# Two fused transformer blocks on one core: a later row piece and sum, stores spread over a stage, and weight chunks at the ends of two attention passes

## The reference

```python
# first block
mod = silu(c) @ w_mod + b_mod                 # 2048 x 12288, one row; six parts
sh1, sc1, g1, sh2, sc2, g2 = split(mod, 6)
h = rmsnorm(x, norm1_w) * (1 + sc1) + sh1
proj = h @ w_in                               # q, k, v, z, xbc, dt, two gates
attn = merge(dilated_window_attention(q, k, v, bias_table, window, dilation) for 3 groups)
y = gated_norm(ssd_chunked(silu(conv(xbc)), dt))
x = x + g1 * ((sig(g_attn) * (attn @ w_attn_proj) + sig(g_ssm) * (y @ w_ssm_proj)) @ w_out)
x = x + g2 * swiglu(rmsnorm(x, norm2_w) * (1 + sc2) + sh2)
x = rmsnorm(x, final_norm_w)
# second block
z = rms_norm(x, ln_gain) @ w_in_2 + b_in_2
y_a = rglru(z.lru_x) * silu(z.lru_gate)
y_b = nsa(q, compressed k/v, selected k/v, window k/v, gates) * silu(z.nsa_gate)
y_c = fox(q, k, v, log_sigmoid(z.fox_f)) * silu(z.fox_gate)
x = x + (sum over the 3 branches of sig(z.merge[i]) * (y_i @ w_branch[i])) @ w_out_2
return x + sig(x @ w_ple_gate) * rms_norm(p @ w_ple, ple_gain)
```

## Time and profile before

| | us |
|---|---|
| median of three runs | 3267.21 |
| the profiled execution's own time | 3268.91 |
| its span, first to last instruction | 3266.7 |
| PE busy | 3198.3 (98%) |
| DVE busy | 2273.8 (70%) |
| ACT busy | 1534.9 (47%) |

### The profile page before, as it was taken

One profiled execution on the slowest core, in us unless ns is written; L12 is line 12 of the kernel. 1 busy time (PEld: TensorE's weight loads), 2 busy tenths in 40 slices (PEclk: granted clock), 3 DMA queues, 4 the chain that ended last, 5 costly groups with the idle time before them and its releaser, 6 DMA issues.

```text
span 3266.7 us, 52356 instructions
## 1 busy us (share of the span) xinstructions
PE 3198.3 (98%) x22201; PEld 2931.7 (90%) x22201; DVE 2273.8 (70%) x2774; ACT 1534.9 (47%) x1560; POOL 0.2 (0%) x4
## 2 busy tenths in 40 slices
PE   8999999999999999999999999999999999999999
PEld 6788989988998898888888888999899999999987
DVE  6697578887787788777776556776555655555676
ACT  3334656634564444433333333476655474434433
POOL 0000000000000000000000000000000000000000
PEclk9999999999999999999999999999999999999999
DMA  9986555565555676566665566554633444455554
GB/s 407 404 350 222 187 191 195 195 260 211 181 181 209 240 271 245 207 220 244 229 225 203 180 202 205 193 178 170 218 141 131 168 168 155 155 182 207 207 191 155
DMA packets 105805, 693.03 MB, mean 212 GB/s; under 512 B 11519, under 2 KB 18751, under 8 KB 30180
## 3 DMA queue, kind: packets, MB, share of 16 engines
q1 hardware_dynamic: 93168, 655.30, 55.3%
q10 hardware_dynamic: 12404, 34.38, 2.8%
HBM read 679.05 MB, written 13.72 MB: 212 GB/s over the span
## 4 chain that ended last, share of the span: by engine, by line
PE 85%; DVE 6%; DMA 4%; ACT 2%; DVEq 2%; issue 1%; SPq 0%; ACTq 0%
PE accp L511 27%; PE accp L512 14%; PE accp L516 12%; PE accp L518 11%; PE accp L517 11%; DVE wlo L1606 2%; DMA raw<-w 2%; PE accp L514 2%; ACT whi L1084 1%; DVE macc L1669 1%; DMA mraw_a<-wm 1%; DVEq L1671 1%; PE pw L1022 1%; PE pw L987 1%; DMA mraw_x<-wm 0%
## 5 line engine op out<-in xcount | busy, mean ns | idle before, releaser
L1606 DVE TENSOR_TENSOR wlo<-raw,whi 128x2048 fp32r<-128x2048 f32 (+1 forms) x544 | 1202.1, 2210 | 498.9 <-ACT whi L1084 493.8
L1084 ACT ACTIVATE whi<-raw 128x2048 fp32r<-128x2048 f32 (+1 forms) x544 | 1003.0, 1847 | 609.0 <-DMA raw<-w 578.2
L511 PE MATMUL accp<-act,whi 128*128 128x512 f32 x2550 | 909.0, 399 | 3.3 <-ACT qkv L1181 1.0
L516 PE MATMUL accp<-act,whi 128*128 128x256 f32 x2912 | 840.5, 289 | 9.5 <-DVE wlo L1606 3.6
L517 PE MATMUL accp<-act,whi 128*128 128x256 f32 x2912 | 824.4, 283 | 0.0
L518 PE MATMUL accp<-act,wlo 128*128 128x256 f32 x2912 | 824.3, 283 | 0.0
L512 PE MATMUL accp<-act,wlo 128*128 128x256 f32 x2720 | 734.8, 280 | 0.0
L511 PEld LDWEIGHTS accp<-act,whi 128*128 128x128 f32 x2550 | 478.9, 188 | 114.4 <-DVE tf L2148 1.4
L516 PEld LDWEIGHTS accp<-act,whi 128*128 128x128 f32 x2912 | 559.0, 192 | 17.6 <-issue 7.3
L517 PEld LDWEIGHTS accp<-act,whi 128*128 128x128 f32 x2912 | 559.2, 192 | 5.3 <-issue 5.0
L518 PEld LDWEIGHTS accp<-act,wlo 128*128 128x128 f32 x2912 | 559.0, 192 | 0.0
(11 more groups left out here) (507 smaller groups left out, 4159.8 us busy)
## 6 DMA issues: line engine op xcount, KB each, us to landing
raw<-w SPq DMA_DIRECT2D x480, 1024.0 KB, 4.8
raw<-w SPq DMA_DIRECT2D x64, 704.0 KB, 4.2
mraw_a<-wm SPq DMA_DIRECT2D x42, 1024.0 KB, 10.4
mraw_b<-wm SPq DMA_DIRECT2D x16, 1024.0 KB, 8.4
mraw_c<-wm SPq DMA_DIRECT2D x16, 1024.0 KB, 6.9
mraw_x<-wm SPq DMA_DIRECT2D x10, 1024.0 KB, 14.1
acb<-ac_d ACTq DMA_DIRECT2D x8, 1024.0 KB, 4.8
mraw_w<-wm SPq DMA_DIRECT2D x8, 1024.0 KB, 7.5
```

Of the source, the lines that this page charges most:

```text
L511: pe.matmul(acc, wh, both, start=first, stop=False, skip_group_check=True)
L516: pe.matmul(acc[:, 0:S], wh, x2[:, 0, :], start=first, stop=False)
L1084: act.activation(whi[:, c % 4, 0:k, :], raw[:, c % 4, 0:k, :], ACT.Copy).then_inc(hi_done, 1)
L1606: dve.tensor_tensor(wlo[:, c % 4, 0:k, :], raw[:, c % 4, 0:k, :], whi[:, c % 4, 0:k, :].bitcast(F32), ALU.subtract).then_inc(lo_done, 1)
```

## The change

**Stage `qs`, PE.** Row piece 3 of the next eighth moves from tile 9 to tile 13, and the sum from tile 13 to tile 17. Pieces 1 and 2 stay at tile 9.

**Stores, ACT.** `e_d` and `bw_d` leave the seventh eighth. `e_d` becomes eight DMAs of 256 KB (2 KB from each partition), and these and the four of `bw_d` are issued one at a time between the splits of the stage `qkv`.

**Second block's attentions, PE and DVE (ACT follows).** In attention a the first riding chunk goes ahead of the second batch's logits, and chunk 23 moves from batch 11 to batch 10. Chunk `ng` 0 goes ahead of the values of batch 10, chunk `ng` 1 between the turn and the values of batch 11; the loop over `ng` starts at 2. In attention b the first riding chunk of DVE moves ahead of the second batch's bias, where PE already had it, and branch chunk 16 goes between the turn and the values of batch 15.

```diff
-        RIDES = {b: [2 * b + 2, 2 * b + 3] for b in range(10)} | {10: [22], 11: [23]}
+        RIDES = {b: [2 * b + 2, 2 * b + 3] for b in range(11)} | {11: []}
...
                     if n < 7 and i == 9:
-                        for j in range(1, 4):
-                            mod_rows(n + 1, j)
+                        mod_rows(n + 1, 1)
+                        mod_rows(n + 1, 2)
                     if n < 7 and i == 13:
+                        mod_rows(n + 1, 3)
+                    if n < 7 and i == 17:
                         mod_block(n + 1)
...
-                    ahead = 1 if b == NSA_B else 0
+                    ahead = 1 if b in (0, NSA_B) else 0
...
+                    if b == NSA_B - 1:
+                        chunk(C0["ng"], E0["ng"], acts)
                     if b > b0:
                         att_values(b - 1)
-                    branch_chunk(ph, rides[-1])
+                    if rides:
+                        branch_chunk(ph, rides[-1])
                     att_turn(b)
+                if ph == "a":
+                    chunk(C0["ng"] + 1, E0["ng"] + 1, acts)
+                else:
+                    branch_chunk("b", 16)
                 att_values(b1 - 1)
...
-                if n == 6:
-                    act.wait_ge(*out_of(8))
-                    act.dma_start(e_d, e0T[:, :, :].rearrange("p k n -> p (k n)")).then_inc(e_st, 16)
-                    for j in range(4):
-                        act.dma_start(bw_d[j], br_d[j:j + 1, :].to_broadcast([P, 1536])).then_inc(brow_st, 16)
             hi(C0["qs"] + 11)
+            act.wait_ge(*out_of(8))
             hi(C0["qkv"])
...
             for c in range(C0["qkv"], C0["dt"]):
                 split_hi(c + 1)
+                j = c - C0["qkv"] - 2
+                if 0 <= j < 16:
+                    if j % 2 == 0:
+                        n = wide(j // 2, 2 * S)
+                        act.dma_start(e_d[:, n], e0T[:, wide(j // 2, 2), :].rearrange("p k n -> p (k n)")).then_inc(e_st, 16)
+                    elif j % 4 == 1:
+                        act.dma_start(bw_d[j // 4], br_d[one(j // 4), :].to_broadcast([P, 1536])).then_inc(brow_st, 16)
-            act.wait_ge(e_st, 16)
+            act.wait_ge(e_st, 128)
...
# DVE, attention
+                    for n in rides[:ahead]:
+                        branch_post(ph, n)
                     if b + 1 < b1:
                         att_bias(b + 1)
                     att_scale(b)
-                    for n in rides[:-1]:
+                    for n in rides[ahead:-1]:
                         branch_post(ph, n)
+                    if b == NSA_B - 1:
+                        split_lo(C0["ng"] + 1)
```

More of the change, by code:

```diff
@@ L1036, in attention @@
                         branch_chunk(ph, n)
+                    if b == NSA_B - 1:
+                        chunk(C0["ng"], E0["ng"], acts)
                     if b > b0:
                         att_values(b - 1)
-                    branch_chunk(ph, rides[-1])
+                    if rides:
+                        branch_chunk(ph, rides[-1])
                     att_turn(b)
+                if ph == "a":
+                    chunk(C0["ng"] + 1, E0["ng"] + 1, acts)
+                else:
+                    branch_chunk("b", 16)
                 att_values(b1 - 1)
             attention(0, NSA_B, "a")
-            for c in range(8):
+            for c in range(2, 8):
                 chunk(C0["ng"] + c, E0["ng"] + c, acts)
@@ L1060, in _ @@
             attention(NSA_B, len(BATCH), "b")
-            for n in range(16, 24):
+            for n in range(17, 24):
                 branch_chunk("b", n)
@@ L1543, in attention @@
                         branch_take(ph, n)
+                    if b == NSA_B - 1:
+                        gate_take("ng", 0)
                     act.wait_ge(aT, 8 + b + 1)
@@ L1553, in _ @@
             attention(0, NSA_B, "a")
-            for t in range(8):
+            for t in range(1, 8):
                 gate_take("ng", t)
@@ L2424, in attention @@
                 for b in range(b0, b1):
+                    rides = RIDES[b]
+                    ahead = 1 if b in (0, NSA_B) else 0
+                    for n in rides[:ahead]:
+                        branch_post(ph, n)
                     if b + 1 < b1:
@@ L2427, in attention @@
                     att_scale(b)
-                    rides = RIDES[b]
-                    for n in rides[:-1]:
+                    for n in rides[ahead:-1]:
                         branch_post(ph, n)
+                    if b == NSA_B - 1:
+                        split_lo(C0["ng"] + 1)
                     if b > b0:
                         att_moved(b - 1)
-                    branch_post(ph, rides[-1])
+                    if rides:
+                        branch_post(ph, rides[-1])
+                if ph == "a":
+                    split_lo(C0["ng"] + 2)
+                else:
+                    branch_post("b", 16)
                 att_moved(b1 - 1)
@@ L2437, in _ @@
             for t in range(8):
-                split_lo(C0["ng"] + t + 1)
+                if t >= 2:
+                    split_lo(C0["ng"] + t + 1)
                 if t == 2:
```

## The result

The changed kernel took 3250.61 us (median of four runs, 3248.83 to 3251.51) against 3267.47 for the kernel before in the same comparison (3266.41 to 3271.1): 16.9 us less, ratio 0.9941 with a 95% interval of 0.993 to 0.9953. Forecast were 14.6 less, 3252.6. In a second comparison it was 3251.61 against 3268.45 (ratio 0.9948, 0.9935 to 0.996). The profiled execution spans 3249.4 us, 17.3 less than before.

The account below looks back on a forecast made before the run. PE was busy 3198.3 of 3266.7 us, with the DMA feed setting the end in `qs` and PE in `qkv`. Terms -4.7 + 0.6 - 3.4 - 6.4 - 0.7 = -14.6 gave 3252.6 us, range 3249 to 3257 (0.55).

Parts of the forecast that it names:

- Stage `qs`: Stage `qs`: later rows and sum, stores gone and the clock kept up, less longer chains, sum to -4.7 us.
- The stores' part: End of `qs`: without the stores in the queue, PE's waits of 2.48 us at 129.07 and 1.04 at 146.29 go.
- The clock's part: `qs` behind the wait at 100 us: full clock instead of partly lower, -1.54 us, called a toss.
- The rows themselves: `qs`: four tiles done ahead win 1.42 us once; the later sum costs 1.2, chunk `qs` 11 0.5, the join 0.1.
- Stores in `qkv`: Stage `qkv`: 5.24 MB of stores want 12.3 us of queue, 8 are free; about 1.0 stall, +0.6 us net.
- the first rival: Stores bind: chunks in `qkv` land after DVE wants them, 5 us of stall rather than 0.6, 3257.0; chance 0.13.
- Start of attention a: Chunk `bra` 2 ahead of the second batch's logits removes waits of 2.22 and 1.51 us; late exponent +0.3; -3.4.
- End of a: Last batches of attention a: `pT` waits go, -3.68 us, low clock behind two, -3.0; softplus +0.3; -6.4.
- Attention b: End of attention b: chunk 16 goes ahead of the wait of 0.69 us at 2845.35, -0.7 us.
- Small packets: Rival in `qkv`: `e_d` in 2 KB rows costs 0.61 us a packet, stall of 38.6 us, 3290.6; chance 0.04.
- the old rate: Rival in `qkv`: the queue carries no more than 352 GB/s, 14.9 us more, 3266.5, no change; chance 0.05.
- that rival: The lower clock comes back elsewhere: all three stretches, 1.54 + 3.0 us, stay, 3257.1; chance 0.15.

Follow-up runs that it names:

- rows alone: Kernel before with only row piece 3 moved to tile 13 and the sum to tile 17: 3268.41 us against 3268.75, ratio 0.9999.
- the stores doubled: Changed kernel with each of the twelve stores issued twice, the second copy to memory nobody reads: 3257.80 us, one run.
- the end undone: Changed kernel with chunks 22 and 23, two `ng` chunks and DVE's splits at the end of attention a back as before: 3257.59 us.
- a burst: Changed kernel with `e_d` stored by one DMA of 2 MB at the place of its first slice: 3252.34 us, one run.

## Why the prediction was right, step by step

**The total** was -14.6 and is -16.9 (-17.4 between the profiles' last products). The mechanism held: no new work, waits removed. By the two profiles 2.8 us came on top of the forecast: 0.9 in the unchanged stretch, which is wander, 1.3 from a to b and 1.3 behind it, less 0.6 that `qkv` cost more and 0.1 in `qs`.

**Stage `qs`, -4.7, measured -4.6.** The sum is right and its split is not; that the errors cancel is luck. The landing of the last third piece came at 124.9 as worked out, and the waits of 2.48 and 1.04 went. The stores' part was forecast at -3.5 and is -4.2 (from 146.29 to 142.09, with the clock low behind 100 us in both profiles). The clock's part, -1.54, came in at -1.4 (142.09 to 140.73, between two kernels that differ in the attentions alone): a toss, as I wrote, that the rows may load, since none of the nine profiles with them lost it. The rows themselves, without the clock, were forecast at +0.4: 1.42 won (4 x 0.36 is 1.44) against 1.8 for the longer chain. Measured is +0.7 to +1.1. So the step "four tiles are now done that came behind it ... won once" holds by itself, and the chain was sized too small: 0.67 an eighth, not 0.4, and 1.2 rather than 0.9 in the last. The whole change to the rows had been booked at -1.2 net, and that is what the runs do not show: rows alone gave 0, and on top of the stores they took 0.7 to 1.1 back wherever the clock held. The longer chain also ate the waits for landings before, at 72 us entirely (1.84 to none) and at 100 us from 2.37 to 0.49, where I wrote 1.8.

**Stores in `qkv`, +0.6, measured +1.2** in the first profile (151.85 to 153.03; 151.74 to 153.13 in four others with this spacing). Without stores in it the stage took 151.85, 152.08 and 151.03, so that the two sizes are not told apart. The price of the bytes was right: 13.4 us of all engines, by 9.0% of 149 us, against 12.3. What I took for slack, 1.3 us at a split, was there only at the head of the stage; at 214.8 DVE had none, and PE's next wait for it came 26 us later. This is the first rival in small. Of the rule from the Trainium skill that I weighed: the stage moved 395 GB/s over 80 us, and 411 from 155 to 255 us with the stores doubled, so a bound of 358 does not hold for this core in this kernel.

**Start of attention a, -3.4, measured -3.8** (339.16 to 335.38 with the end undone). The 0.3 for a late exponent did not come.

**End of a, -6.4, measured -7.3:** waits 3.68 and two low stretches of 3.4 us at half clock, 1.7 each, so 3.4 rather than 3.0. The 0.3 behind the softplus did not come: the wait is 0.71 as it was.

**Attention b, -0.7, measured -2.0** (-1.4 in the second profile). The wait for `pT` at 2845 went (0.7), and the wait of 0.23 for `wlo` at 2750 that I had left aside went as well. The wait for DVE at the branch's end wanders: 0.62 before, 0.27 and 0.97 in the changed kernel's two profiles. The stretch took 558.8 to 559.3 in the three profiles with the old attention b and 556.6 to 557.6 in the eleven with the new: 1.2 to 2.7 less, of which 0.9 is traced to waits.

**The rivals.** Small packets are refuted by the row of 1728 packets, the old rate by the window of 395. The clock did come back once elsewhere, at 2339.5, in the changed kernel's first profile and cost it 1.5 (a stretch near there, 2335 to 2343 us, stands in six of the fourteen profiles, two of them with all attentions as before); in its second it came at 430.6. So that rival had its share right as a hazard, not as a rule.

## What to carry to other kernels

Before one waits for what comes late one should ask what sets its lateness: moving the consumer down gained nothing while a store filled the queue, and after the store was gone it cost up to 1.1 us, or paid 0.3 to 0.7 where it kept the clock up. A store that must share a full stage goes in thin slices over the whole stage, since a late chunk stops the engine that has no slack (`qkv` took 151.0 us with thin slices, 154.9 with a burst). And a softmax at the end of a pass wants work from the next stage beside it: three waits of 3.7 us in all were worth 7.3, because the clock fell behind two of them.

## What was not expected of the hardware

The lower clock came in stretches of 3.4 us, or of 6.8 or 10.2, in every profile: one to five of them ahead of the last product, always one that began between 35.9 and 38.9 us, others at different places in executions of the same code. The waits of 1.04 and 1.95 us at the end of attention a brought two of them in two profiles and one in the two others. The waits of 2.3 to 2.5 us near 100 us brought one in two profiles (2.37 and 2.52) and none in two others (2.28 and 2.29); near 72 us one of 1.72 was followed by 6.8 us of it, and those of 1.84, 1.84, 2.26 and 2.28 in the four other profiles by none. What tells the cases apart stays open. Together with other wander it moves a stretch of 2060 us of unchanged code by up to 6 us from one execution to the next, more than most of the single edits here are worth.
